# Modulation of the first norm by quarters of K, half of each block on TensorE

## The reference

```
c_act = silu(c)
mod = c_act @ ada_w[i] + ada_b[i]              # (2048) x (2048, 12288)
sh1, sc1, g1, sh2, sc2, g2 = split(mod, 6)
h = x * (1.0 + sc1) + sh1
q, k, v, z, b, a, u = split(h @ w_in, ...)     # u: the S5 channels, b and a: gate logits
ya = gated_deltanet(q, k, v, z, b, a, ...)
yb = s5_ssm(u, ...)                            # a scan over the tokens
x = layer_norm(ALPHA * x + (1.0 + g1) * (concat(ya, yb) @ w_out), ...)
h = x * (1.0 + sc2) + sh2; y = swiglu(h); x = layer_norm(ALPHA * x + (1.0 + g2) * y)
```

## Time and profile before

| | us |
|---|---|
| median of 3 runs (range) | 2773.31 (2766.16 to 2775.39) |
| the profiled execution | 2767.55 |
| its span | 2765.9 |
| TensorE matmul busy | 2542.9 (92%) |
| VectorE busy | 2046.9 (74%) |
| ScalarE busy | 1220.4 (44%) |
| mean granted clock of TensorE | 0.953 of full |

### The profile page before, as it was taken

One profiled execution on the slowest core, in us unless ns is written; L12 is line 12 of the kernel. 1 busy time (PEld: TensorE's weight loads), 2 busy tenths in 40 slices (PEclk: granted clock), 3 DMA queues, 4 the chain that ended last, 5 costly groups with the idle time before them and its releaser, 6 DMA issues.

```text
span 2765.9 us, 41894 instructions
## 1 busy us (share of the span) xinstructions
PE 2542.9 (92%) x16532; PEld 2298.9 (83%) x16532; DVE 2046.9 (74%) x2518; ACT 1220.4 (44%) x1614; POOL 197.5 (7%) x226
## 2 busy tenths in 40 slices
PE   1499998888889999999999899998999999999998
PEld 1488777777878899889988799998878998899887
DVE  8879999778587777777778888568887655555556
ACT  1255555544455433443343453453464434443444
POOL 0012332000000000000001011000000000000000
PEclk8589999888899999999999899999999999999998
DMA  9874444556448788888888499556588665555652
GB/s 374 285 254 143 152 151 149 195 172 203 138 153 302 272 276 275 277 280 278 277 274 291 154 335 337 173 168 219 183 276 280 214 195 186 190 190 184 196 184 77
DMA packets 272987, 616.02 MB, mean 223 GB/s; under 512 B 23211, under 2 KB 23746, under 8 KB 272578
## 3 DMA queue, kind: packets, MB, share of 16 engines
q1 hardware_dynamic: 240020, 488.00, 52.2%
q0 software_dynamic: 32640, 125.84, 13.0%
q10 hardware_dynamic: 174, 0.04, 0.0%
HBM read 611.73 MB, written 2.10 MB: 222 GB/s over the span
## 4 chain that ended last, share of the span: by engine, by line
PE 74%; DVE 17%; issue 3%; DMA 3%; ACT 2%; SPq 2%; DVEq 0%; POOL 0%; POOLq 0%
PE groups L2530 11%; PE groups L2534 11%; PE groups L2532 11%; PE groups L2538 10%; PE groups L2542 10%; PE groups L2540 10%; DMA ada_units<-in_ada_w_dram 3%; DVE ada_acc L2032 2%; DVE w_lo L2050 2%; SPq L1659 1%; PE pc L2709 1%; DVE ada_acc L872 1%; PE pb L2699 1%; DVE ada_acc L2357 1%; PE groups L1131 1%
## 5 line engine op out<-in xcount | busy, mean ns | idle before, releaser
L1749 ACT ACTIVATE w_hi<-w_raw 128x1024 fp32r<-128x1024 f32 x776 | 817.3, 1059 | 1136.1 <-PE groups L2534 544.6
L2050 DVE TENSOR_TENSOR w_lo<-w_raw,w_hi 128x1024 fp32r<-128x1024 f32 x747 | 905.5, 1223 | 530.4 <-ACT w_hi L1749 526.4
L2530 PE MATMUL groups<-w_hi,act_hi 128*128 128x512 f32 x1408 | 553.4, 393 | 19.8 <-DVE act_lo L2184 19.8
L2534 PE MATMUL groups<-w_lo,act_hi 128*128 128x512 f32 x1408 | 549.9, 391 | 0.0
L2532 PE MATMUL groups<-w_hi,act_lo 128*128 128x512 f32 x1408 | 549.9, 391 | 0.0
L2538 PE MATMUL groups<-act_hi,w_hi 128*128 128x256 f32 x1776 | 511.6, 288 | 33.3 <-DVE act_lo L2184 13.9
L2540 PE MATMUL groups<-act_lo,w_hi 128*128 128x256 f32 x1776 | 503.1, 283 | 0.0
L2542 PE MATMUL groups<-act_hi,w_lo 128*128 128x256 f32 x1776 | 503.0, 283 | 0.0
L2538 PE MATMUL groups<-hid_hi,w_hi 128*128 128x256 f32 x1392 | 390.6, 281 | 0.0
L2542 PE MATMUL groups<-hid_hi,w_lo 128*128 128x256 f32 x1392 | 388.9, 279 | 0.0
L2540 PE MATMUL groups<-hid_lo,w_hi 128*128 128x256 f32 x1392 | 388.9, 279 | 0.0
(11 more groups left out here) (440 smaller groups left out, 2498.6 us busy)
## 6 DMA issues: line engine op xcount, KB each, us to landing
ada_units<-in_ada_w_dram POOLq DMA_DIRECT2D x120, 1024.0 KB, 6.5
w_raw<-in_ffn_w_gate_dram SPq DMA_DIRECT2D x88, 1024.0 KB, 5.2
w_raw<-in_ffn_w_up_dram SPq DMA_DIRECT2D x88, 1024.0 KB, 5.3
w_raw<-in_ffn_w_down_dram SPq DMA_DIRECT2D x88, 1024.0 KB, 5.1
w_raw<-in_cd_w_in_dram SPq DMA_DIRECT2D x48, 1024.0 KB, 5.8
w_raw<-in_ab_w_in_dram SPq DMA_DIRECT2D x40, 1024.0 KB, 5.8
ada_units<-in_ada_w_dram SPq DMA_DIRECT2D x80, 512.0 KB, 4.4
w_raw<-in_ab_w_out_dram SPq DMA_DIRECT2D x16, 1024.0 KB, 6.0
```

Source lines behind the costliest of these rows:

```text
L1749: act.activation(whi[:, half, k], raw[:, slot, k], ACT.Copy).then_inc(hi_done, 1)
L2050: dve.tensor_tensor(wlo[:, half, k], raw[:, slot, k], whi[:, half, k].bitcast(F32), ALU.subtract).then_inc(lo_done, 1)
L2530: pe.matmul(dst, hi[:, k, rows], whi[:, j % 2, kk], start=(k == 0), stop=False, skip_group_check=True)
L2534: last = pe.matmul(dst, hi[:, k, rows], wlo[:, j % 2, kk], start=False, stop=(k == UK * p["units"] - 1), skip_group_check=True)
```

## The change

The eight blocks of the first norm are made by quarters of K of the product that follows: quarter q is one block of shift and one of scale, the 512 columns that the K tiles 4q to 4q+3 of h need. Loads are units of 512 by 512 (rows of 2 KB), numbered m = 0 to 39, eight a quarter. Even m go to VectorE (four steps of 512 columns, `head_ada` there), odd m to TensorE: sixteen products of one column, weight tile by a column of `c_act`, added up in PSUM (`head_ada` of the tensor program), and `head_total` adds VectorE's part with a column of ones. Loads 0 to 7 have buffers of their own, 8 to 31 go through a ring of five. After each quarter its activations are made (`head_take`, `head_h`), and the two units of `in0u` that read them stand in TensorE's stream between the one-column products of the next quarter; their loads stand in SP's queue between the modulation loads. Logits stand between units 6 and 7. The S5 weight tiles, the copies of the groups and DeltaNet's gate terms stand behind unit 7 on TensorE and ScalarE.

Blocks 8 and 9 (m = 32 to 39) move from beside `in0u` (and from GpSimd's queue) into `in0`: loads on SP at `HEAD_LATE`, VectorE's four units in slots 1, 3, 5, 7, TensorE's in 2, 4, 6, 8, the sum in slot 9, the taking in slot 10. `EARLY_AT` moves to slots 15 to 31. The small parameters have three semaphores instead of one.

```diff
-ADA_FIRST = 4
+HEAD_BLOCKS = 10
+HEAD_LOADS = 4 * HEAD_BLOCKS
+HEAD_RING = 5
 FIRST_SLOTS = 8
 ADA_FREE = 4 * (FIRST_SLOTS - 1) + 1
 TWO_PI_LOW = 6.283185
-N_VEC_LOADS, N_PAR_LOADS = 19, 23
...
+HEAD_BUFFER = [m if m < FIRST_SLOTS else (4 + FIRST_SLOTS - 4 if (m - FIRST_SLOTS) % HEAD_RING == 4 else (m - FIRST_SLOTS) % HEAD_RING)
+               if m < 32 else m % 2 for m in range(HEAD_LOADS)]
+HEAD_BEFORE = [max([n for n in range(m) if HEAD_BUFFER[n] == HEAD_BUFFER[m]], default=None) for m in range(HEAD_LOADS)]
+HEAD_USE = [sum(HEAD_BUFFER[n] == HEAD_BUFFER[m] for n in range(m)) + 1 for m in range(HEAD_LOADS)]
+HEAD_LATE = {2: 32, 3: 33, 6: 34, 7: 35, 8: 36, 9: 37, 10: 38, 11: 39}
...
+            def head_load(m):
+
+                q, r = m // 8, m % 8
+                block, j = (q + 4 * (r // 4) if q < 4 else 8 + r // 4), r % 4
+                before = HEAD_BEFORE[m]
+                if before is not None:
+                    sp.wait_ge(*((head_used, before // 2 + 1) if before % 2 else (head_step, UK * (before // 2 + 1))))
+                elif HEAD_BUFFER[m] == FIRST_SLOTS:
+                    sp.wait_ge(vec_turned, len(VECS))
+                sp.dma_start(head_slots[HEAD_BUFFER[m]], ada_w[0][UK * P * j:UK * P * (j + 1), GROUP * block:GROUP * (block + 1)]
+                             .rearrange("(k p) n -> p k n", p=P)).then_inc(ada_in_first[HEAD_BUFFER[m]], 16)
...
+            in0u = by_name["in0u"]
+            load(vrow[0:16, 4], c[0].rearrange("(t p) -> t p", p=P), vec_in)
+            head_loads(0, 2)
...
+            head_loads(2, 4)
+            load(xrow[:], x[0].rearrange("(t p) d -> p t d", p=P), x_in)
+            head_loads(4, 8)
+            for j in (0, 1):
+                weight_unit(in0u, 0, j)
+            for q in range(1, 4):
+                for half in range(2):
+                    head_loads(8 * q + 4 * half, 8 * q + 4 * half + 4)
+                    if 2 * q + half < 7:
+                        weight_unit(in0u, 0, 2 * q + half)
+
...
-        EARLY_AT = (4, 5, 7, 11, 12, 13, 15, 19, 20, 21, 23, 27, 28, 29, 30, 31)
+        EARLY_AT = (15, 16, 17, 18, 19, 20, 21, 23, 24, 25, 26, 27, 28, 29, 30, 31)
...
+            def head_ada(m):
+
+                q, r, d = m // 8, m % 8, m // 2
+                b, j = r // 4, r % 4
+                if q and j == 0:
+                    dve.wait_ge(head_sums, q)
+                dve.wait_ge(ada_in_first[HEAD_BUFFER[m]], 16 * HEAD_USE[m])
+                for kk in range(UK):
+                    k, unit = UK * j + kk, head_slots[HEAD_BUFFER[m]][:, kk]
                     if k == 0:
-                        last = dve.tensor_scalar(total, unit, cact[:, 0:1], None, ALU.mult)
+                        last = dve.tensor_scalar(acc[:, b], unit, cact[:, 0:1], None, ALU.mult)
                     else:
-                        dve.wait_ge(ada_step, 32 * i + 2 * k + ADA_FREE)
-                        last = dve.scalar_tensor_tensor(total, unit, cact[:, k:k + 1], total, ALU.mult, ALU.add)
-                    last.then_inc(ada_step, 2)
-                    if k == 4 and i:
-                        take_first(i - 1)
-
-            def take_first(i):
-                dve.wait_ge(ada_summed, 2 * i + 3)
-                cols = slice(2 * GT * i, 2 * GT * i + 2 * GT)
-                dve.tensor_tensor(mod[:, cols], pm[:, 0:2 * GT], adab[:, cols], ALU.add).then_inc(mod_taken, 2)
-
-            ada_first(0)
+                        dve.wait_ge(head_step, UK * d + kk)
+                        last = dve.scalar_tensor_tensor(acc[:, b], unit, cact[:, k:k + 1], acc[:, b], ALU.mult, ALU.add)
+                    last.then_inc(head_step, 1)
+
+            def head_take(q):
+
+                dve.wait_ge(head_sums, q + 1)
+                sums = (pc if q % 2 else pm)[:, 0:2 * GT]
+                if q == 4:
+                    dve.tensor_tensor(mod[:, 32:40], sums, adab[:, 32:40], ALU.add).then_inc(mod_taken, HEAD_BLOCKS)
+                    return
+                both = lambda cols: cols[:, 0:32].rearrange("p (b k) -> p b k", b=2)[:, :, 4 * q:4 * q + 4]
+                link(dve.tensor_tensor(both(mod), sums.rearrange("p (b k) -> p b k", b=2), both(adab), ALU.add))
+                dve.tensor_scalar(fold[:, 0, 4 * q:4 * q + 4], mod[:, KT + 4 * q:KT + 4 * q + 4], 1.0, 1.0 / ALPHA, ALU.add,
+                                  ALU.mult).then_inc(head_mod, 1)
...
+            for m in range(0, 8, 2):
+                head_ada(m)
...
+            head_take(0)
+            dve.wait_ge(x_taken, 8)
+            head_h(0)
...
+            split_lo(1, 1, 1)
...
+                head_ada(8 * q)
+                head_ada(8 * q + 2)
+                split_lo((2 * q) % 4, 0, 2 * q)
+                head_ada(8 * q + 4)
+                head_ada(8 * q + 6)
+                head_take(q)
+                head_h(q)
+                split_lo((2 * q + 1) % 4, 1, 2 * q + 1)
+            split_lo(0, 0, 8)
+            deltanet_set_dve(dve, 2)
+            deltanet_set_dve(dve, 4)
...
+                n = 8 * i + j
+                if n in (1, 3, 5, 7):
+                    head_ada(31 + n)
+                if n == 10:
+                    head_take(4)
+                    dve.sem_inc(ada_step, KT * HEAD_BLOCKS)
+                    dve.sem_inc(ada_summed, HEAD_BLOCKS)
+                deltanet_early_dve(dve, n)
...
+            def head_ada(m):
+
+                q, r = m // 8, m % 8
+                pe.wait_ge(c_done, 1)
+                pe.wait_ge(ada_in_first[HEAD_BUFFER[m]], 16 * HEAD_USE[m])
+                if q > 1:
+                    pe.wait_ge(head_mod, q - 1)
+                for kk in range(UK):
+                    k = UK * (r % 4) + kk
+                    for t in range(GT):
+                        at = GT * (r // 4) + t
+                        last = pe.matmul((pc if q % 2 else pm)[:, at:at + 1], head_slots[HEAD_BUFFER[m]][:, kk, P * t:P * t + P], cact[:, k:k + 1],
+                                         start=(r == 1 and kk == 0 and t == 0), stop=False, skip_group_check=True)
+                last.then_inc(head_used, 1)
+
+            def head_total(q):
+
+                pe.wait_ge(head_step, 4 * UK * (q + 1))
+                for b in range(2):
+                    for t in range(GT):
+                        at = GT * b + t
+                        last = pe.matmul((pc if q % 2 else pm)[:, at:at + 1], acc[:, b, P * t:P * t + P], ones[:, 0:1], start=False, stop=True,
+                                         skip_group_check=True)
+                last.then_inc(head_sums, 1)
...
+            head_ada(5)
+            head_ada(7)
+            head_total(0)
...
+            for q in range(1, 4):
+                head_ada(8 * q + 1)
+                head_unit(2 * q - 2)
+                head_ada(8 * q + 3)
+                head_unit(2 * q - 1)
+                head_ada(8 * q + 5)
+                head_ada(8 * q + 7)
+                head_total(q)
+            head_unit(6)
+            logits()
+            head_unit(7)
+            pe.wait_ge(s5_setd.sem, s5_setd.at(0, "done"))
+            pe.wait_ge(s5c_in, 16 * N_S5C_LOADS)
+            for t in range(HT):
+                s5_weights(t)
+            pe.wait_ge(s5_wtaken, HT)
+            deltanet_set_pe(pe)
...
+                if n in (2, 4, 6, 8):
+                    head_ada(31 + n)
+                if n == 9:
+                    head_total(4)
```

233 lines of the change are left out of this document (117 added, 116 removed).

## The result

The changed kernel is slower: a median of 2825.34 us over 4 runs (2815.95 to 2830.39), beside 2772.02 us for the kernel before on the same chip. The ratio is 1.0198, with a 95% interval of 1.0182 to 1.0213, so the change costs 1.8 to 2.1%, some 55 us by the ratio (53 by the medians).

A forecast was written before the change was run, and what follows sets the result against it. Modulation-weight loads were taken to bound the head, with VectorE's limit close. An anchor 15.9 us earlier and slots 12.9 us longer summed to -3.0 us: 2764.6 profiled, 2770.3 as median of runs, range 2758 to 2784.

The forecast's parts named there:

- sixteen take 1.84 us at full clock, 3.58 at half: Head, TensorE: price of sixteen one-column products, read from rows of the earlier trace.
- TensorE's 26.0 us: Head: TensorE's work per quarter, 26.0 us, just under the 27.0 us of loads, so loads stay the bound.
- The loads: Head: 39 MB at 388 GB/s take 105.4 us, 27.0 us a quarter; last landing at 116 us.
- one of the signs that I had named for being wrong: Head: the forecast is wrong if the DMA share falls under 0.9.
- The tail: Head, from last sums at 121.5 to the first S5 recurrence step at 171.6, instead of 187.45 before.
- The clock: Head, TensorE: half clock in one-column and narrow products, rising about 3 us after dense products begin; dense unit 7.8 us.
- Rival 3: Head: clock stays half in dense units, TensorE bounds at 36.4 us a quarter; +30 us, 2803; chance 0.08.
- Rival 2: Slots: VectorE's and TensorE's additions do not overlap, +20 instead of +12.9; head gains 13; +7, 2780; chance 0.16.
- Rival 1: Head does better: loads at 410 GB/s (-5), warmer narrow work (-5); -13 us, 2760; chance 0.22.
- The slots: First dense stage's 32 slots: +8.8 us from late modulation units and +4.1 from moved steps, together +12.9.
- TensorE ran ahead during the long odd slot: Even slots: TensorE's added 1.9 us counts only in slot 2; from slot 4 on it can run ahead.
- The moved steps: Slots: six accumulation steps move later; 5.5 us gained where they leave, up to 9.6 paid where they enter, +4.1.

The follow-up runs named there:

- after: The changed kernel as profiled, against the kernel before: median 2825.34 us over 4 runs, ratio 1.0198.
- drop_cols: Changed kernel without fifteen of sixteen one-column products in each TensorE head unit of the first eight modulation blocks: 2775.94 us, ratio 1.0028 to before.
- contig: Changed kernel with each quarter's two dense units first and the four one-column units after them on TensorE: 2835.05 us, ratio 1.0237 to before.
- early_at: Kernel before with only the early accumulation steps moved to slots 15 to 31, as the change does: 2773.86 us, ratio 1.0015.

## Why the prediction was wrong

- **The step that failed** is the price in "sixteen take 1.84 us at full clock, 3.58 at half". Those rows are eight products. Per quarter the forecast paid 3.6 + 1.9 + 2 x 2.8 = 11.1 us for four one-column units and 1.4 for the sums; the chain of after shows 6.83 + 3.46 + 10.04 = 20.3 and 3.41. The dense units, forecast 13.5, took the other 15.2. So TensorE's 26.0 us are 39.0 in fact, and 11.2 of these 13 us are the mis-sized price. It was the term nearest to a limit: 26.0 against the loads' 27.0, so nearly all of the miss came through as time: the last take is at 163.99 where 122 was forecast. The code gave the count. The rows gave a hint: 0.118 us is the distance of two dense products of 256 columns, and 1.84 / 16 is 0.115 for one column, the same distance for what I took to be a whole float32 product.
- **The loads** were right: with the products away the third quarter is 27.0 us at 386 GB/s, and the last take at 121.45 where 121.5 was forecast. In the changed kernel itself their share falls to 0.69 to 0.83, one of the signs that I had named for being wrong, because the ring then waits for TensorE.
- **The tail** from the last sums to the anchor was 50.1 us in the forecast; it is 48.2 in after and 48.5 in `drop_cols`. Right within 2 us, S5's scaling included, which lay beside the eighth unit as said, but for 1.25 us that TensorE waited for its end.
- **The clock** behaved in the head as assumed, half in two of four one-column units and full in much of the dense ones. It multiplies the price: an estimate from the rows with everything at full clock is 4 x 3.63 + 1.84 + 96 x 0.118 = 27.7 us for a quarter, so half clock is some 11 of the 39.0 us. The forecast had counted its clock (26.0 where the same sum at full clock gives 19.8), but on half the instructions. As a difference between two orders it is small: 0.9 us net a quarter in `contig`.
- **Rival 3** had the right engine, the right sign and the right point of decision ("as soon as a quarter of TensorE's work passes 27.0 us"), and 36.4 us a quarter where 39.0 came, but its reason was dense units at half clock. The chain shows that only in part: the dense units take 15.2 us, where they would take 20.4 all at half clock and 11.3 all at full. 0.08 was its chance for that reason. The forecast's error was in the term that both shared. Rival 2's mechanism, additions on the two engines that do not overlap, came true in the even slots, at more than its price; its gain in the head did not. Rival 1 did not come.
- **The slots.** For slots 1 to 8 the forecast had +8.8; against the base of `early_at` it is 27.5 in after (30.1 with slots 0 and 9). VectorE's part was right: slots 3, 5 and 7 grew by 2.95, 2.3 and 2.97 us (forecast 2.4, 2.1, 2.4), at 10.8 to 11.1 us. TensorE's part was not: "TensorE ran ahead during the long odd slot" would have hidden three of four units. No trace shows that: slots 2, 4, 6 and 8 grew by 18.3 us in after and by 11.0 to 17.4 in the four other kernels with the same slots. Four units at full clock are 14.5 us; what comes on top in after goes with the clock, which falls to half within the unit and stays there for the small products behind (283.62 to 293.2 in the rows of slot 6). The moved steps were right: +4.8 against +4.1.
- In sum, 24.8 + 35.0 = 59.8 us at slot 31, of which 57.2 reach the end of the span.

The Trainium skill bears on the failed step. FP8 and Floating Point Precision, in TensorE Precision Notes, says that true FP32 takes four passes through the array. The trace agrees that one such product is more than one instruction and shows two, each with its weight load; an estimate by that page, four times the 0.115 us of one instruction, would be 29 us for a quarter's 64 products at full clock, against 14.5 (4 x 3.63) in the rows. For the cost the measurement decides: two instructions and half of that estimate. How many passes one instruction makes, no run here shows. The page would have warned of the term, though.

On the clock, TensorE: Matmul & The Clock Gate, Part 1, says that activity releases the throttle. In after TensorE was busy without a gap from 46.7 to 163.8 us and the granted clock was 0.68 on average. Its level follows the kind of work in these stretches (0.50 and 1.00 before the DMA share are its two levels, 1.2 and 2.4 GHz):

```profile
64.00:70.00 6.00, 6.00 (x29) 6.00 (x29) 5.27 (x8) 0.00 (x0) 0.00 (x0) 0.50 1.05 388
72.00:76.00 4.00, 4.00 (x39) 4.00 (x38) 0.00 (x0) 0.00 (x0) 0.00 (x0) 1.00 1.03 378
```

64 to 70 are dense products behind a one-column unit (60.88 to 64.66), and from 73.12 on it is one-column products behind dense ones. In both stretches the level is the one that fits the work before it. Activity alone, read plainly as being busy, does not keep the full clock here.

## What to carry to other kernels

Before a row with a count is used as a price, tie the count to the loop in the code: operands in float32 make two instructions of each product, and a price that is off by two is worst where the sum stands just under the bound. Narrow products are paid by the instruction, not by the column (one and eight columns cost the same here), and TensorE's clock falls during them, also for what comes behind; the cheapest are single units directly behind dense work. One trace of each kernel is not enough to compare stretches in which this happens: slots with the same instructions differed by 7 us in all. Two engines that split a chain of work gain only until the faster one waits for the hand-over: here six loads to two was better by 28 us than four to four.

## What was not expected of the hardware

- A float32 matmul of 128x128 by one column is two weight loads and two matmuls: 0.227 us at full clock (3.63 / 16), 0.437 at half (6.99 / 16). With eight columns it is the same. A float32 transpose of 128x128 is one instruction (x32 for 32 in the earlier trace rows).
- The granted clock falls to half while TensorE is busy without a gap, if what it does are one-column products: 4.89 us for a unit begun at full clock in slot 6, and a mean of 0.68 over 117 us in which such units and dense ones take turns.
- Rows of 2 KB load at 386 GB/s over a whole quarter, as the single stretch of the earlier trace rows had it.
